# FFN up projection: nine seven-product pairs per layer in groups of three, instead of seven in periods of two

## The reference

```python
def conv_ffn(x, w_up, conv_w, conv_b, w_down):      # x: 512 x 1024, w_up: 1024 x 5632
    h = x @ w_up
    h = causal_depthwise_conv(h, conv_w, width=3) + conv_b
    gate, val = jnp.split(h, 2, axis=-1)            # 2816 features each
    return (jax.nn.silu(gate) * val) @ w_down
```

## Time and profile before

| | us |
|---|---|
| median of 3 runs | 2041.09 |
| lowest, highest | 2038.85, 2041.33 |
| the profiled execution's own time | 2042.29 |
| its span, first to last instruction | 2040.6 |
| mean granted clock of TensorE | 1.000 |

### The profile page before, as it was taken

The page is one execution under the profiler, slowest core; times in us unless marked ns, Lnnn a source line. Parts: engine busy times, 40 slices in busy tenths (PEclk is TensorE's granted clock), DMA queues, the critical chain, the costliest instruction groups (busy, mean ns, idle before and its releaser), DMA issues.

```text
span 2040.6 us, 33333 instructions
## 1 busy us (share of the span) xinstructions
PE 2026.4 (99%) x12636; PEld 1750.7 (86%) x12636; DVE 1619.3 (79%) x2555; ACT 1115.0 (55%) x1861; POOL 433.7 (21%) x482
## 2 busy tenths in 40 slices
PE   9999999999999999999999999999999999999998
PEld 8889998888988899888877888998888889999887
DVE  6668878889467887899888669777997668877898
ACT  4755545447335555546656646555465755545555
POOL 0520332210000232120035402322110520332220
PEclk9999999999999999999999999999999999999999
DMA  8123344384432334467421123334674122334393
GB/s 291 64 104 125 109 130 150 121 255 172 145 129 75 97 105 129 145 190 243 166 73 42 63 83 104 119 104 155 197 237 163 65 104 83 109 122 147 115 269 122
DMA packets 82570, 276.42 MB, mean 135 GB/s; under 512 B 9408, under 2 KB 13632, under 8 KB 82032
## 3 DMA queue, kind: packets, MB, share of 16 engines
q1 hardware_dynamic: 59184, 214.67, 30.4%
q0 software_dynamic: 11200, 24.12, 5.8%
q10 hardware_dynamic: 12032, 35.54, 4.8%
HBM read 256.43 MB, written 14.73 MB: 133 GB/s over the span
## 4 chain that ended last, share of the span: by engine, by line
PE 91%; DVE 5%; DMA 2%; ACT 1%; issue 0%; DVEq 0%; ACTq 0%; SPq 0%
PE ps L2437 12%; PE ps L2438 12%; PE ps L2439 12%; PE ps L2649 6%; PE ps L3018 5%; PE ps L3019 5%; PE ps L3020 5%; PE ps L2976 5%; PE ps L2978 5%; PE ps L2977 5%; PE ps L2509 2%; PE ps L2465 2%; PE ps L2466 2%; PE ps L2467 2%; DMA raw<-slabs 2%; PE ps L2497 1%
## 5 line engine op out<-in xcount | busy, mean ns | idle before, releaser
L2437 PE MATMUL ps<-h_hi,w_hi 128*128 128x512 f32 (+1 forms) x1104 | 433.0, 392 | 0.0
L2438 PE MATMUL ps<-h_lo,w_hi 128*128 128x512 f32 (+1 forms) x1104 | 429.6, 389 | 0.0
L2439 PE MATMUL ps<-h_hi,w_lo 128*128 128x512 f32 (+1 forms) x1104 | 428.9, 389 | 0.0
L1603 DVE TENSOR_TENSOR w_lo<-raw,w_hi 128x1024 fp32r<-128x1024 f32 x300 | 372.0, 1247 | 39.1 <-ACT w_hi L901 35.5
L901 ACT ACTIVATE w_hi<-raw 128x1024 fp32r<-128x1024 f32 x312 | 326.4, 1053 | 133.1 <-DVE raw L2251 74.0
L2437 PEld LDWEIGHTS ps<-h_hi,w_hi 128*128 128x128 f32 x1104 | 207.6, 188 | 44.0 <-issue 4.0
L2439 PEld LDWEIGHTS ps<-h_hi,w_lo 128*128 128x128 f32 x1104 | 207.3, 188 | 43.2
L2438 PEld LDWEIGHTS ps<-h_lo,w_hi 128*128 128x128 f32 x1104 | 207.7, 188 | 38.9
L1281 ACT ACTIVATE work<-ps,conv_sb 128x512 f32<-128x512 f32 x120 | 93.0, 775 | 162.6 <-PE ps L2439 133.2
L3018 PE MATMUL ps<-w_hi,h_hi 128*128 128x512 f32 x408 | 159.7, 391 | 2.1 <-DVE w_lo L1603 2.1
L3020 PE MATMUL ps<-w_hi,h_lo 128*128 128x512 f32 x408 | 158.8, 389 | 0.0
(11 more groups left out here) (365 smaller groups left out, 5054.6 us busy)
## 6 DMA issues: line engine op xcount, KB each, us to landing
raw<-slabs SPq DMA_DIRECT2D x368, 512.0 KB, 4.1
act<-slabs POOLq DMA_DIRECT2D x64, 256.0 KB, 5.6
bias<-slabs SPq DMA_DIRECT2D x16, 512.0 KB, 6.3
x_dram<-x ACTq DMA_DIRECT2D x16, 512.0 KB, 5.0
x<-x_dram ACTq DMA_DIRECT2D x16, 512.0 KB, 4.9
raw<-act POOLq DMA_DIRECT2D x28, 256.0 KB, 3.3
act<-slabs SPq DMA_DIRECT2D x12, 512.0 KB, 5.4
bias_dram<-bias_rows ACTq DMA_DIRECT2D x2, 2048.0 KB, 12.3
```

What stands on the lines that cost most here:

```text
L1603: ve.tensor_tensor(w_lo[:, c % RING, :], raw[:, raw_slot(c), :], w_hi[:, c % RING, :].bitcast(f32), ALU.subtract).then_inc(lo_made, 1)
L2437: pe.matmul(ps[:, bank, cols], hi, h_hi[:, k, cols], start=k == 0, stop=False)
L2438: pe.matmul(ps[:, bank, cols], hi, h_lo[:, k, cols], start=False, stop=False)
L2439: last = pe.matmul(ps[:, bank, cols], lo, h_hi[:, k, cols], start=False, stop=k == KT - 1)
```

## The change

Pairs 4, 6, 7, 9, 10, 12, 13, 15 and 16 are now seven-product pairs. Pair 4 with the ordinary pair 5 keeps the old order (`first_period`). Pairs 6 to 17 form four groups of three, (f, g, n) = (6, 7, 8), (9, 10, 11), (12, 13, 14), (15, 16, 17): f and g by seven products, n ordinary. On TensorE a group runs P1 P2 P6 P5 P7 of f, P1 P2 of g, P4 P3 of f, P6 P5 P7 of g, the even slab of n, P4 P3 of g, the odd slab of n. All pairs from 4 to 17 take turns in four sets of two banks. The lists of VectorE, ScalarE, GpSimd and SP are rewritten to match, and waits count products and parts in the new order. `X1_ORDER` says that x1's parts of g are made before those of f. SP's list is now simply pair after pair, even and odd. What is computed stays as it is. The core of the diff (hunks on helper names and counters left out; in the lists of ScalarE and VectorE the removed `period` is left out, as it stands above):

```diff
-FASTS = (FAST_END - FAST) // 2
+GROUPS_OF_THREE = 6, 9, 12, 15
+FAST_PAIRS = [FAST] + [q + e for q in GROUPS_OF_THREE for e in range(2)]
+FASTS = len(FAST_PAIRS)
+X1_ORDER = [FAST] + [q + e for q in GROUPS_OF_THREE for e in (1, 0)]
+UP_PRODUCTS = [(FAST, p) for p in (1, 2, 6, 4, 3)] + [
+    (q + e, p) for q in GROUPS_OF_THREE
+    for e, p in ((0, 1), (0, 2), (0, 6), (1, 1), (1, 2), (0, 4), (0, 3), (1, 6), (1, 4), (1, 3))]
 PARTS = "a11", "x1", "x2", "x3", "x4"
 STEPS = FFT // 2
...
         def up_bank(q, e):
-            return (0 if q // 2 % 2 else 4) + e
+            return 2 * ((q + 2) % 4 if FAST <= q < FAST_END else q % 2) + e
         def sum_place():
...
@@ -707,24 +729,19 @@
                         sp.wait_ge(at_added, 2 * DOUBLES)
                     early_slabs(n1)
                 ring_slabs(n1 + EARLY, up_slab(L, FAST))
-                for q in range(FAST, FAST_END + 2, 2):
+                for q in range(FAST, FAST_END + 1):
                     for e in range(2):
                         c = up_slab(L, q, e)
-                        if q == FAST:
+                        if q - 2 not in FAST_PAIRS:
                             sp.wait_ge(lo_made, made(c - RAW))
                         elif e:
-                            sp.wait_ge(part_lo_made["x3"], fast(L, q - 2) + 1)
-                            sp.wait_ge(part_lo_made["x4"], fast(L, q - 2) + 1)
+                            sp.wait_ge(part_lo_made["x3"], part_count(L, q - 2, "x3"))
+                            sp.wait_ge(part_lo_made["x4"], part_count(L, q - 2, "x4"))
                         else:
-                            sp.wait_ge(part_lo_made["x1"], fast(L, q - 2) + 1)
+                            sp.wait_ge(part_lo_made["x1"], part_count(L, q - 2, "x1"))
                             sp.wait_ge(up_x2, fast(L, q - 2) + 1)
                             sp.wait_ge(up_x3, fast(L, q - 2) + 1)
                         sp.dma_start(raw[:, raw_slot(c), :], slabs[dram(c)]).then_inc(raw_in[raw_slot(c)], 16)
-                    if q < FAST_END:
-                        for e in range(2):
-                            c = up_slab(L, q + 1, e)
-                            sp.wait_ge(lo_made, made(c - RAW))
-                            sp.dma_start(raw[:, raw_slot(c), :], slabs[dram(c)]).then_inc(raw_in[raw_slot(c)], 16)
                 ring_slabs(up_slab(L, FAST_END + 1), DOWN[L] + FFT)
                 for j in range(STEPS):
                     if j == RAW and L + 1 < DEPTH:
...
                 elif kind == 2:
                     at_probs(BASE[L])
-                fourth_sum(L, FAST)
-                for j in range(STEPS - 1):
+                fourth_sum(L, 4)
+                down_sums(L, 0)
+                down_sums(L, 1)
+                fourth_sum(L, 6)
+                fourth_sum(L, 7)
+                down_sums(L, 2)
+                fourth_sum(L, 9)
+                down_sums(L, 3)
+                fourth_sum(L, 10)
+                down_sums(L, 4)
+                fourth_sum(L, 12)
+                fourth_sum(L, 13)
+                down_sums(L, 5)
+                fourth_sum(L, 15)
+                down_sums(L, 6)
+                fourth_sum(L, 16)
+                for j in range(7, STEPS - 1):
                     down_sums(L, j)
-                    if FAST <= 2 * j + 4 < FAST_END and j:
-                        fourth_sum(L, 2 * j + 4)
                 first_sums(L)
...
                     sc.wait_ge(w_used, 4 * i + (c - (RING + EARLY if early(c - RING) else RING) + 1))
+                if isinstance(i, int) and in_fast(c - RING):
+                    L, q, e = in_fast(c - RING)
+                    sc.wait_ge(up_mm, product_count(L, q, 2 if e else 3))
                 if isinstance(i, int) and summed(c):
                     L = max(k for k in range(DEPTH) if DOWN[k] <= c)
...
                         sc.wait_ge(w_used, up_slab(L, q) + 2)
                     else:
-                        sc.wait_ge(up_mm, 5 * fast(L, q) + (1, 3)[n])
+                        sc.wait_ge(up_mm, product_count(L, q, (1, 6)[n]))
                     if q > FAST:
-                        sc.wait_ge(up_c, 3 * fast(L, q - 2) + (1, 3, 2)[n])
+                        sc.wait_ge(up_c, 3 * (fast(L, q) - 1) + (1, 3, 2)[n])
                     sc.activation(kept_sum(n), ps[:, up_bank(q, 0), 0:HALF], ACT.Copy).then_inc(up_copy, 1)
                 def part_hi(q, name):
...
-
+                def first_period(q):
+                    slab_tap(q - 1, 1)
                     part_hi(q, "x3")
                     copy(q, 0)
                     split_hi(up_slab(L, q + 1))
+                    slab_silu(q - 1)
                     split_hi(up_slab(L, q + 1, 1))
                     copy(q, 1)
                     part_hi(q, "x4")
                     copy(q, 2)
+                    part_hi(q + 2, "a11")
+                    part_hi(q + 2, "x2")
+                    slab_tap(q, 0)
+                    part_hi(q + 3, "x1")
+                    part_hi(q + 2, "x1")
+                    slab_tap(q, 1)
+                    slab_silu(q)
+                    slab_tap(q + 1, 0)
+                def period(f):
+                    g, n = f + 1, f + 2
+                    more = n + 1 < FAST_END
+                    slab_tap(f - 1, 1)
+                    part_hi(f, "x3")
+                    copy(f, 0)
+                    part_hi(g, "a11")
+                    slab_silu(f - 1)
+                    copy(f, 1)
+                    part_hi(f, "x4")
+                    copy(f, 2)
+                    part_hi(g, "x2")
+                    copy(g, 0)
+                    part_hi(g, "x3")
+                    slab_tap(f, 0)
+                    split_hi(up_slab(L, n))
+                    slab_tap(f, 1)
+                    copy(g, 1)
+                    slab_silu(f)
+                    split_hi(up_slab(L, n, 1))
+                    part_hi(g, "x4")
+                    copy(g, 2)
+                    if more:
+                        part_hi(f + 4, "x1")
+                        slab_tap(g, 0)
+                        part_hi(f + 3, "a11")
+                        part_hi(f + 3, "x2")
+                        slab_tap(g, 1)
+                        part_hi(f + 3, "x1")
                     else:
                         sc.dma_start(x[:, 0, :], x_dram[0]).then_inc(x_back, 16)
                         sc.dma_start(x[:, 1, :], x_dram[1]).then_inc(x_back, 16)
                         operand(L, 0)
                         for j in range(4):
                             s1(L, j)
+                        slab_tap(g, 0)
                         sc.dma_start(x[:, 2, :], x_dram[2]).then_inc(x_back, 16)
                         sc.dma_start(x[:, 3, :], x_dram[3]).then_inc(x_back, 16)
+                        split_hi(up_slab(L, n + 1))
+                        slab_tap(g, 1)
+                        split_hi(up_slab(L, n + 1, 1))
+                    slab_tap(n, 0)
+                    slab_silu(g)
...
@@ -2084,6 +2163,7 @@
                     ve.wait_ge(raw_in[row1], raw_count(up_slab(L, q, 1)))
                     if q > FAST:
                         ve.wait_ge(part_lo_made["x2"], fast(L, q))
+                        ve.wait_ge(up_x3, fast(L, q))
                         ve.wait_ge(up_x4, 16 * fast(L, q))
                     ve.tensor_tensor(sum_place(), raw[:, row2, 0:SEQ], raw[:, row1, 0:SEQ], ALU.add).then_inc(up_x2, 1)
...
+                def first_period(q):
                     slab_taps(q - 1, 1)
                     split_lo(up_slab(L, q + 1))
+                    slab_gate(q - 1)
                     split_lo(up_slab(L, q + 1, 1))
                     c11(q)
                     part_lo(q, "x4")
                     c22(q)
+                    x1(q + 2)
+                    x2(q + 2)
+                    x1(q + 3)
+                    part_lo(q + 2, "a11")
+                    part_lo(q + 2, "x2")
+                    slab_taps(q, 0)
+                    c12(q)
+                    part_lo(q + 3, "x1")
+                    part_lo(q + 2, "x1")
+                    slab_taps(q, 1)
+                    x3(q + 2)
+                    slab_gate(q)
+                def period(f):
+                    g, n = f + 1, f + 2
+                    more = n + 1 < FAST_END
+                    slab_tap(f - 1, 0, 1)
+                    if f > GROUPS_OF_THREE[0]:
+                        part_lo(f, "x1")
+                    slab_tap(f - 1, 1, 1)
+                    slab_tap(f - 1, 0, 0)
+                    part_lo(f, "x3")
+                    slab_tap(f - 1, 1, 0)
+                    part_lo(g, "a11")
+                    slab_gate(f - 1)
+                    x2(g)
+                    c11(f)
+                    c22(f)
+                    part_lo(f, "x4")
+                    part_lo(g, "x2")
+                    x3(g)
+                    part_lo(g, "x3")
+                    slab_tap(f, 0, 1)
+                    c12(f)
+                    slab_tap(f, 0, 0)
```

(90 more changed lines are left out.)

124 lines of the change are left out of this document (55 added, 69 removed).

## The result

The changed kernel takes 2084.9 us in the median (2083.96 to 2085.87), the kernel before 2041.0 on the same chip. The ratio is 1.0219, 95% interval 1.0205 to 1.0233: 44 us slower. The sign was forecast, the size was not: +23 was predicted, 2046 to 2078 the range.

A forecast was written before the change was run, and what follows sets the result against it. TensorE's own issue was taken as the bound. 24 us for twelve steps, 2.4 contention and 4 for later mean landings, less 7.0 gained, gave +23: 2064 us, from the shown runs' median of 2041.1, range 2046 to 2078.

The forecast's parts named there:

- The gain: TensorE in the up projection: each converted pair saves 0.88 us, eight pairs 7.0 us if TensorE never waits.
- First step, the wait on the slab: Between groups of three, VectorE sits idle 4.2 us before x1(f+4), waiting for the even slab's load.
- Second step, what is queued behind it: VectorE's work behind the late x1(f+4) makes TensorE 2.0 us late per step between groups, twelve steps, 24 us.
- X: The time VectorE starts x1(f+4), put at 24.75 us after the start of P1(f).
- the chain: VectorE's in-order work from x1(f+4) on, which makes TensorE wait at P5, P7 and P1: 24 us.
- late landings: Slab loads between groups: the mean landing is later than the usual one, 12 x 0.35 = 4 us.
- The first step of a layer: From pair 4 to group 6: same load wait, but low a11(7) comes 0.3 us before its P1; cost 0.
- Contention with GpSimd: Sums beside VectorE's low x1 and x3 in steps between groups: 8 x 0.3 = 2.4 us, bounds 0 and 0.9.
- Rival (d): Full lock-out by GpSimd: each of 8 exposed steps waits for about one more operation, 10 us more, 2074; chance 0.10.
- (a): Rival: the second slab is there when VectorE asks, TensorE never waits, only the 7.0 us stay: 2034; chance 0.12.
- (b): Rival: steps between groups cost only 0.6 us each as handovers overlap better, about the same time, 2041; chance 0.06.
- (c): Rival: slabs land 5.0 to 6.0 us after issue as a rule, 1.3 us more per step, 2076; chance 0.12.

The follow-up runs named there:

- run 6: Changed kernel with the edits of run 5 and run 3 together: 2036.0 us, 0.9979 of the kernel before.
- run 4: Changed kernel with the edits of run 1 and run 3 together: 2036.0 us, 0.9974 of the kernel before.
- run 3: Changed kernel, in SP's list the load of g's even slab goes ahead of f's odd one for groups 9, 12 and 15: 2050.7 us.
- run 8: Changed kernel with run 1's edit, and x1(g) with its parts made in its own group from group 9 on, loads unmoved: 2047.2 us.
- run 2: Changed kernel, all GpSimd sums over finished pairs work on 2 of their 256 columns: 2059.4 us.
- run 9: Changed kernel, in groups 6 and 12 GpSimd waits for c22(f) before issuing the accumulating DMA of x4(g): 2066.0 us.
- run 5: Changed kernel, in groups 6 and 12 GpSimd runs the finished pair's sums ahead of the accumulating DMA issue of x4(g): 2065.4 us.
- run 1: Changed kernel, GpSimd's sums in groups 6 and 12 wait until c12(f) is done, the DMA issue not moved: 2070.1 us.
- run 7: Kernel before, GpSimd's sums of a finished pair put right behind the accumulating DMA of the same period: 2041.8 us, ratio 1.0004.

## Why the prediction was wrong, step by step

- **The gain, 7.0 us for eight pairs: right.** In run 6 products keep 1.44 us, ordinary slabs 5.47, a group takes 31.08. The medians of runs 4 and 6 lie 4.4 to 5.1 us under the kernel before (in the trace of run 6 the four regions are 583.2 us long, before 588.4, so 5.2 of the 7.0); waits before P6(6) take 0.9 us of the rest.
- **First step, the wait on the slab: right.** VectorE's idle time before x1(f+4) was put at 4.2 us, 4.5 at the mean; it is 4.82 and 4.32 in the first two steps of layer 0. Run 3 took the wait away and with it 34.2 us.
- **Second step, what is queued behind it: right on VectorE, wrong on what TensorE waits for, and the size met in part by luck.** From X on the chain is met to 0.2 us. But the walk left ScalarE out ("10.89 of 21.00 leaves it room"), and low parts were to show before P5, P7 and P1(g). Of the 31.7 us that the two lines of waits name, 23.6 go to ScalarE's copies; in the changed kernel P5(f) loses 0.1 us instead of 1.0, P6(f) loses 0.9 to 1.1 for copy(f, 0), and P1(f) up to 1.3 where it was to be in time. The two ways happen to give nearly the same delay: in the step to group 9 low x1(9) ends at 265.60, and P5(9), held up by P6(9), starts at 265.66. Both come from the same late VectorE, since runs 3 and 8 remove both; no run changes ScalarE's list. The chain alone was priced at 24 us, 28 with late landings; run 2 shows 21.3 in the twelve steps and 23.8 over the four regions. With sums beside it I had 30.4 us; in run 9 the four regions last 154.1, 152.1, 153.2 and 152.7 us, 31.3 us over the undisturbed ones. Run 9's 2066.0 and run 5's 2065.4 lie at the 2064 that was predicted, which is luck in part, since two errors cancel: the chain with its late landings was put too high (28), and the sums beside the steps, at 2.4, too low: 31.3 - 23.8 = 7.5.
- **The first step of a layer at 0: right in three layers.** In layer 0 TensorE waited 1.0 us before P6(6). That is the place where a load landed 5.5 us after its issue in the kernel before; no run tested it further.
- **Contention with GpSimd: this is the step that failed.** "I take 0.3 each, 8 x 0.3 = 2.4 us; bounds 0 and 0.9". Measured: 18.9 us (run 9) and 19.5 (run 5) for the lock-out in groups 6 and 12 alone, seven places out of eight, 2.7 us each: 0.7 to 0.9 before P3(f), 0.9 before P7(g), the rest because VectorE is late at x4(g) and so the slab is asked for later (low x4(7) is done 2.04 us ahead of P4(7), in run 9 2.87). I looked for sums beside parts only in the steps between groups, and took the price from a row in which VectorE had merely met a sum halfway. I read `fourth_sum(L, 7)` followed by `down_sums(L, 2)` in the new list for whether GpSimd would be late, not for what it would hold. The bounds were wrong with it: nothing in the rows allowed an upper bound of 0.9 for two engines that can hold each other for several operations.
- **Rival (d)** named the cause, but at 10 us more and in other places. With its full price in groups 6 and 12 the forecast would have been about 2083. The rule of the Trainium skill that was weighed (SBUF — State Buffer, Who interferes with whom) says that the engine that is second waits for the first one's whole instruction. Here both directions show: VectorE held 3.60 us in the changed kernel, GpSimd held 2.17 us in run 5. But VectorE waited through four operations of GpSimd, not one, and GpSimd's copy lasted until three of VectorE's were through.
- **Rivals (a), (b), (c):** the slab did not arrive in time, the steps did not shrink to 0.6 us, and the landings were not 5 to 6 us as a rule.

What stays open: why an issue of the accumulating DMA with sums right behind it lets GpSimd keep VectorE out over four operations, while sums alone do not. That the sums are needed is shown by runs 1 and 2. That the issue is needed rests on run 5, which also moves the sums in time, and on the traces, in which every hold of this kind has an issue right ahead of the sums. One difference shows in the rows: behind an issue GpSimd's operations start 0.33 to 0.35 us before the end shown of the one before (235.12 to 236.85 above), while the copy behind the sum at 263.79 starts 0.05 before it. Whether that is the reason is not shown.

## What to carry to other kernels

A spare share of an engine is worth only what its in-order list lets it use: walk one steady period, find the instruction that waits for the last load of a queue, and put that load or that instruction elsewhere; here exchanging two entries of a load list, three times a layer, was worth 34 us. When work is repacked more tightly, a delay that slack had swallowed (2.35 to 2.68 us for a 1.2 us operation in run 7, at no cost) comes out at full price. Walk the lists of all engines that TensorE waits for: a copy that needs 0.4 us was late because of what stood ahead of it. Where VectorE and GpSimd both read SBUF, look for work of GpSimd right behind a DMA issue and for what VectorE starts in the 3 us after it: a semaphore that puts GpSimd second is cheap and was worth 19 us. With both mended, the nine pairs in groups of three are 0.2 to 0.3% faster than the kernel before.

## What the runs showed of the hardware that was not expected

- A VectorE subtraction of 512 columns with two inputs from SBUF took 3.60 us instead of 0.69 when GpSimd had issued a DMA 0.28 us before and went on with sums. With the sums gone (run 1) or the issue 0.39 us after VectorE's start (run 9) it took 0.68.
- The hold ends at a fixed time: 33 operations of VectorE that started 0.27 to 2.9 us behind such an issue ended 3.9 us (512 columns) or 4.4 to 4.5 us (1024) behind it (changed kernel, runs 3, 7 and 9). Additions in PSUM and taps, which read PSUM and SBUF, kept their 0.42 and 0.75 us beside the same sums in run 7.
- In the reverse case GpSimd's copy of 256 columns took 2.17 us (run 5) while VectorE ran three such operations back to back at 0.69 each.
- Whether a place is hit depends on a few tenths of a microsecond: seven of eight like places were hit in one execution of the changed kernel, the eighth was not, where VectorE began 0.25 us behind the issue and not 0.27 or 0.28; in run 3 all eight were.
